# How expert rows come back to their tokens: shares applied at eviction, gathers that add, and two scatters into the output

## The reference, cut to what matters

```python
x = x + jnp.einsum('bsd,de->bse', merged, w_out[l])
h2 = rms_norm(x, norm2_gain[l])
x = x + hierarchical_moe(h2, ...)
...
top_val, top_idx = lax.top_k(e_sel_logits, TOP_K_IN_GROUP)
top_w = jax.nn.softmax(top_val, axis=-1) * g_w
combine_w = jnp.sum(jax.nn.one_hot(expert_id, N_EXPERTS) * top_w[..., None], axis=1)
...
hid = jax.nn.silu(a) * u * cs[:, :, None]
return jnp.einsum('nef,efd->nd', hid, w_down)
```

## Time and profile before

| | us |
|---|---|
| median of 3 runs | 1813.12 |
| lowest and highest | 1811.01, 1814.26 |
| profiled execution, its own time | 1811.73 |
| its span in the profile | 1809.9 |
| PE busy | 1748.1 |
| DVE busy | 1179.7 |
| ACT busy | 887.3 |
| POOL busy | 349.4 |

### The profile page before, as it was taken

One profiled execution on the slowest core, in us unless ns is written; L12 is line 12 of the kernel. 1 busy time (PEld: TensorE's weight loads), 2 busy tenths in 40 slices (PEclk: granted clock), 3 DMA queues, 4 the chain that ended last, 5 costly groups with the idle time before them and its releaser, 6 DMA issues.

```text
span 1809.9 us, 25327 instructions
## 1 busy us (share of the span) xinstructions
PE 1748.1 (97%) x10148; PEld 1438.6 (79%) x10148; DVE 1179.7 (65%) x1700; ACT 887.3 (49%) x1411; POOL 349.4 (19%) x228
## 2 busy tenths in 40 slices
PE   8999999999999999999999999999999999999993
PEld 6998788999897677788999776765568868888882
DVE  5575644554466655555776598586774466888896
ACT  5425434334334544334343365556653366878881
POOL 3323222001242322001000276310010030000001
PEclk8999999999999999999999999999999999999997
DMA  6203111323311212323222210112233349999984
GB/s 190 77 24 100 48 48 51 110 74 111 97 64 54 70 47 71 101 94 98 94 92 73 70 48 24 55 62 93 70 139 129 132 177 389 410 415 409 401 350 174
DMA packets 121279, 241.31 MB, mean 133 GB/s; under 512 B 9593, under 2 KB 101018, under 8 KB 115018
## 3 DMA queue, kind: packets, MB, share of 16 engines
q1 hardware_dynamic: 113786, 212.88, 33.2%
q0 software_dynamic: 4464, 16.25, 2.4%
q10 hardware_dynamic: 2912, 10.55, 1.4%
HBM read 223.41 MB, written 16.25 MB: 132 GB/s over the span
## 4 chain that ended last, share of the span: by engine, by line
PE 51%; DVE 5%; ACT 4%; issue 1%; DMA 1%; POOL 0%; POOLq 0%; ACTq 0%; DVEq 0%
PE acc L1409 15%; PE acc L880 10%; PE acc L1124 9%; PE acc L1149 7%; PE acc L1213 3%; PE acc L1227 2%; PE acc L1244 1%; PE acc L1235 1%; PE acc L1109 1%; PE acc L1393 1%; DVE upad L2751 1%; DVE qk L2751 1%; ACT v L2008 1%; PE acc L1031 0%; DVE qk L2749 0%
## 5 line engine op out<-in xcount | busy, mean ns | idle before, releaser
L880 PE MATMUL acc<-h_split,ring_split 128*128 128x264 f32 (+1 forms) x864 | 269.4, 312 | 0.0
L880 PEld LDWEIGHTS acc<-h_split,ring_split 128*128 128x128 f32 x864 | 162.3, 188 | 9.7
L1149 PE MATMUL acc<-ring_split,h_split 128*128 128x256 f32 x384 | 107.9, 281 | 0.0
L880 PE MATMUL acc<-h_split,qk_split 128*128 128x264 f32 (+1 forms) x288 | 92.6, 322 | 1.3 <-DVE ring_split L2255 1.3
L880 PE MATMUL acc<-ring_split,qk_split 128*128 128x264 f32 (+1 forms) x288 | 92.2, 320 | 0.0
L2255 DVE TENSOR_TENSOR ring_split<-ring,o_split 128x1024 fp32r<-128x1024 f32 (+1 forms) x32 | 44.8, 1415 | 64.3 <-ACT o_split L1570 64.2
L3067 POOL TENSOR_TENSOR latent<-latent 128x528 f32<-128x528 f32 x18 | 26.8, 1490 | 292.8 <-ACT latent L1565 292.4
L2255 DVE TENSOR_TENSOR ring_split<-ring,qk_split 128x1024 fp32r<-128x1024 f32 (+1 forms) x56 | 59.4, 1069 | 34.0 <-ACT qk_split L1570 34.0
L880 PE MATMUL acc<-h_split,krope_split 128*128 128x264 f32 (+1 forms) x240 | 79.4, 331 | 1.9 <-POOL ring_split L3081 1.9
L3081 POOL TENSOR_TENSOR ring_split<-ring,krope_split 128x1024 fp32r<-128x1024 f32 x20 | 48.1, 2406 | 152.4 <-ACT krope_split L1570 152.4
L880 PE MATMUL acc<-ring_split,krope_split 128*128 128x264 f32 (+1 forms) x240 | 77.0, 321 | 0.0
(11 more groups left out here) (599 smaller groups left out, 5579.2 us busy)
## 6 DMA issues: line engine op xcount, KB each, us to landing
ring<-in_w_in SPq DMA_DIRECT2D x64, 1024.0 KB, 5.3
ring<-in_w_expert_gate SPq DMA_DIRECT2D x10, 2048.0 KB, 11.1
ring<-in_w_expert_up SPq DMA_DIRECT2D x10, 2048.0 KB, 10.1
ring<-in_w_expert_down SPq DMA_DIRECT2D x10, 2048.0 KB, 10.6
ring<-in_w_out SPq DMA_DIRECT2D x12, 1024.0 KB, 5.2
y_rows<-gate ACTq DMA_DIRECT2D x16, 512.0 KB, 10.3
hres<-in_w_expert_up SPq DMA_DIRECT2D x3, 2048.0 KB, 10.3
qk<-in_w_expert_down SPq DMA_DIRECT2D x3, 2048.0 KB, 11.3
```

Source lines behind the costliest of these rows:

```text
L880: ins = nc.tensor.matmul(dst[0:rows_, half, 0:x.shape[1]], w[:, k, :], x, start=(k == 0 and i == 0), stop=(k == last and i == 2), skip_gro ...
L1149: ins = nc.tensor.matmul(dst[:, side, 0:WIDE], x[k][:, rows_], w, start=(k == 0 and part == 0), stop=(k == DC - 1 and part == 2), skip_gro ...
```

## The change: what it does

- The results are scaled by their shares when ACT evicts them: a factor for each slot (`R_WS`), made by eight matmuls on PE in turn 0 (`slot_weights`) and copied by DVE.
- The results of experts 0 to 13 (`FETCHED` of them) go to `y_rows` as before. `back_rows` is now worked out by DVE in turn 5 (`rows_fetched`); a result that isn't among these rows points to a tile of zeros. POOL, once the store of expert 13 has landed, issues four gathers for the tokens' first results and four for the second, each adding its rows to `x_tok` in place; a second one waits for the first of the same tile. SP then stores the four tiles to `out`. There is no DVE work in the combine.
- The results of experts 14 and 15 (`ADDED`) are not stored to `y_rows`. When the four stores to `out` have landed, POOL adds them from SBUF to rows of `out` by an indirect DMA that adds (a scatter), one after the other, each waited for. Their rows (`added_rows`) come from eight matmuls on PE in turn 4; the slots left free point to tokens of other experts, each a different one, with a share of 0.
- To that end the places of all tokens for all experts are worked out in turn 1. ACT evicts expert 13 at the start of turn 14, ahead of three `weights_up`. The hidden rows of expert 15 and its result get buffers of their own (`last_up`, `last_low`, `y_last`); the transposes of expert 15 come between the two halves of the down product of expert 14.
- The tile of zeros is one store instead of seven. The overflow loop also adds into `out`.

The core of the diff:

```diff
+ADDED = 2
+FETCHED = EXPERTS - ADDED
...
@@ SP
+            for i in range(QT):
+                sp.wait_ge(rows_back[i], 32)
+                sp.dma_start(out[0, i * P:(i + 1) * P, :], x_tok[:, i, :]).then_inc(stored, 16)
...
@@ PE
-                out_of_hidden(e)
+                out_of_hidden(e, range(1) if e == EXPERTS - 2 else range(2))
+
+            def slot_weights():
+                pe.wait_ge(dve_made, at(dve_made, "by_choice"))
+                for j in range(2):
+                    for i in range(QT):
+                        at_ = R_BY + 64 * j + 16 * i
+                        ins = nc.tensor.matmul(BANK["pick"][:, 0:EXPERTS], picks_whole[j][:, i, :].bitcast(F32), R[:, at_:at_ + EXPERTS],
+                                               start=(j == 0 and i == 0), stop=(j == 1 and i == QT - 1))
+                done(ins, "slot_weights")
+
+            def rows_added():
+                for x in range(ADDED):
+                    pe.wait_ge(dve_made, at(dve_made, ("added_pick", x)))
+                    for i in range(QT):
+                        ins = nc.tensor.matmul(BANK["pick"][:, 32 + x:33 + x], picks[x][:, i, :], late(K_TOKEN + i, 1),
+                                               start=(i == 0), stop=(i == QT - 1))
+                done(ins, "added_rows")
...
+                if e == 0:
+                    slot_weights()
+                if e == 4:
+                    rows_added()
                 down_of(e)
             hidden_of(EXPERTS - 1)
+            out_of_hidden(EXPERTS - 2, range(1, 2))
             down_of(EXPERTS - 1)
...
@@ ACT
                 act.wait_ge(psum_filled, at(psum_filled, ("y", e)))
-                if e:
+                if e == 0:
+                    act.wait_ge(dve_made, at(dve_made, "slot_weights"))
+                elif e <= FETCHED:
                     act.wait_ge(y_main, 16 * e)
-                evacuated(nc.scalar.activation(y_out, acc[:, 2, :, :].rearrange("p a b -> p (a b)"), ACT.Copy),
-                          ("y", e))
+                evacuated(nc.scalar.activation(y_out if e < EXPERTS - 1 else y_last,
+                                               acc[:, 2, :, :].rearrange("p a b -> p (a b)"), ACT.Copy,
+                                               scale=R[:, R_WS + e:R_WS + e + 1]), ("y", e))
+                if e >= FETCHED:
+                    return
...
+                if e == FETCHED:
+                    expert_out(e - 1)
                 weights_up(j + 2)
                 weights_up(j + 3)
                 weights_up(j + 4)
                 expert_gated(e + 1)
                 hidden_up(e)
-                if e:
+                if e and e < FETCHED:
                     expert_out(e - 1)
...
@@ DVE
                 weights_low(j + 6)
+                if e == EXPERTS - 2:
+                    hidden_low(EXPERTS - 1)
                 weights_low(j + 7)
-            hidden_low(EXPERTS - 1)
...
+                if e == 0:
+                    slot_weights()
+                elif e == 1:
+                    places_of_all()
+                elif e - 2 < ADDED:
+                    added_pick(e - 2)
+                elif e == 4:
+                    added_rows_kept()
+                elif e == 5:
+                    rows_fetched()
...
-            for i in range(QT):
-                dve.wait_ge(rows_back[i], 32)
-                for j in range(2):
-                    ins = stt(out=x_tok[:, i, :], in0=returned[:, 2 * i + j, :],
-                              scalar=R[:, R_WT + 4 * j + i:R_WT + 4 * j + i + 1], in1=x_tok[:, i, :],
-                              op0=ALU.mult, op1=ALU.add)
...
@@ POOL
+            pool.wait_ge(dve_made, at(dve_made, "back_rows"))
+            pool.wait_ge(act_evacuated, at(act_evacuated, ("x_tok", QT - 1)))
+            pool.wait_ge(y_zeroed, 16)
+            pool.wait_ge(y_main, 16 * FETCHED)
+            for j in range(2):
+                for i in range(QT):
+                    if j:
+                        pool.wait_ge(rows_back[i], 16)
+                    nc.gpsimd.indirect_dma_start(x_tok[:, i, :], None, y_rows,
+                                                 bass.IndirectOffsetOnAxis(back_rows[:, 4 * j + i:4 * j + i + 1], 0),
+                                                 compute_op=ALU.add).then_inc(rows_back[i], 16)
+
+            def add_rows(rows, source):
+
+                nc.gpsimd.indirect_dma_start(out[0], bass.IndirectOffsetOnAxis(rows, 0), source, None,
+                                             compute_op=ALU.add).then_inc(y_added, 16)
+
+            pool.wait_ge(stored, 16 * QT)
+            pool.wait_ge(dve_made, at(dve_made, "added_rows"))
+            for x in range(ADDED):
+                pool.wait_ge(act_evacuated, at(act_evacuated, ("y", FETCHED + x)))
+                add_rows(added_rows[:, x:x + 1], y_out if x < ADDED - 1 else y_last)
+                mark(y_added, None, 16)
+                pool.wait_ge(y_added, 16 * (x + 1))
...
-            pool.wait_ge(all_stored, 1)
-            for i in range(QT):
-                for j in range(2):
-                    nc.gpsimd.indirect_dma_start(returned[:, 2 * i + j, :], None, y_rows,
-                                                 bass.IndirectOffsetOnAxis(back_rows[:, 4 * j + i:4 * j + i + 1], 0))\
-                        .then_inc(rows_back[i], 16)
```

More of the change, by code:

```diff
@@ L1448, in out_of_hidden @@
                         ins.then_inc(first_half, 1)
-                done(ins, ("y", e))
+                if half == 1:
+                    done(ins, ("y", e))
             def weights_of(name):
@@ new lines, in _, with slot_weights, places_of_all @@
+            places = r(R_Q, QT, 16)
+            tokens_of = late(K_TOKEN, QT).unsqueeze(2).to_broadcast([P, QT, 16])
+            def slot_weights():
+                dve.wait_ge(psum_filled, at(psum_filled, "slot_weights"))
+                made(nc.vector.tensor_copy(R[:, R_WS:R_WS + EXPERTS], acc[:, 3, 1, 0:EXPERTS]), "slot_weights")
+            def places_of_all():
+                counts = R[:, R_P + 64:R_P + 80].unsqueeze(1).to_broadcast([P, QT, 16])
+                chain(stt(out=places, in0=r(R_P, QT, 16), scalar=-2.0, in1=tokens_of, op0=ALU.mult, op1=ALU.add))
+                chain(tt(places, places, counts, ALU.add))
+                chain(ts(R[:, R_V:R_V + 64], R[:, R_M:R_M + 64], -1.0, 1.0, ALU.mult, ALU.add))
+                chain(tt(R[:, R_Q:R_Q + 64], R[:, R_Q:R_Q + 64], R[:, R_V:R_V + 64], ALU.mult))
+                chain(tt(R[:, R_Q:R_Q + 64], R[:, R_Q:R_Q + 64], R[:, R_P:R_P + 64], ALU.add))
@@ new lines, in added_pick, with added_rows_kept, rows_fetched @@
+            def added_pick(x):
+                e = FETCHED + x
+                made(pick(picks[x], places[:, :, e:e + 1]), ("added_pick", x))
+            def added_rows_kept():
+                dve.wait_ge(psum_filled, at(psum_filled, "added_rows"))
+                made(nc.vector.tensor_copy(added_rows[:, :], acc[:, 3, 1, 32:32 + ADDED]), "added_rows")
+            def rows_fetched():
+                base, ok, row = (R[:, x:x + 8] for x in (R_S, R_S + 8, R_WT))
+                own, slot = late(K_TOKEN, 1), R[:, R_SLOT:R_SLOT + 8]
+                first = late(K_FIRST, 16).unsqueeze(1).to_broadcast([P, 8, 16])
+                chain(tt(r(R_KEY, 8, 16), r(R_SEL[0], 8, 16), first, ALU.mult))
+                chain(nc.vector.tensor_reduce(base, r(R_KEY, 8, 16), AX.X, ALU.add))
+                chain(ts(ok, slot, float(P), None, ALU.is_lt))
+                chain(stt(out=ok, in0=base, scalar=float(FETCHED * P), in1=ok, op0=ALU.is_lt, op1=ALU.mult))
+                chain(stt(out=row, in0=base, scalar=-float(FETCHED * P + 1), in1=slot, op0=ALU.add, op1=ALU.add))
+                chain(ts(row, row, own, None, ALU.subtract))
+                chain(tt(row, row, ok, ALU.mult))
+                chain(ts(row, row, own, float(FETCHED * P), ALU.add, ALU.add))
+                made(nc.vector.tensor_copy(back_rows[:, :], row), "back_rows")
@@ L3018, in _ @@
             with dve.If(tiles > 0):
+                which = R[:, R_TW:R_TW + 2 * QT].rearrange("p (i x) -> p i x", x=2)
+                chain(nc.vector.tensor_copy(which[:, :, 0:1], late(K_TOKEN, QT).unsqueeze(2)))
                 with dve.Fori(0, tiles) as k:
@@ L3022, in _ @@
                     mine = R[:, R_A:R_A + 4]
+                    chain(nc.vector.tensor_copy(which[:, :, 1:2], r(R_W, QT, 16)[:, :, bass.ds(expert, 1)]))
                     chain(nc.vector.tensor_copy(mine.unsqueeze(2), places[:, :, bass.ds(expert, 1)]))
@@ L3026, in _ @@
                     dve.wait_ge(psum_filled, at(psum_filled, ("pick", "+")))
+                    dve.wait_ge(y_added, at(y_added, ("y", "+"), back=1))
+                    chain(nc.vector.tensor_copy(R[:, R_WP:R_WP + 1], acc[:, 3, 1, 1:2]))
                     made(nc.vector.tensor_copy(rows_of[:, 0:1], acc[:, 3, 1, 0:1]), ("rows_of", "+"))
@@ L3181, in _ @@
             chain(nc.gpsimd.memset(padf[:, 0:D], 0.0))
```

(4 more changed lines are left out.)

100 lines of the change are left out of this document (33 added, 67 removed).

## The result

The change made the kernel slower. The changed kernel's median is 1819.3 us (1814.57 to 1823.52, 20 runs) against 1812.92 us (1808.9 to 1815.62, 20 runs) of the kernel before on the same chip: ratio 1.0035, 95% interval 1.0026 to 1.0043, or 6.4 us. The forecast was 1808.4 us and faster. The profiled execution took 1821.06 us, with a span of 1819.1.

What follows compares the result with a forecast made beforehand. PE bounds the kernel before 1770, then a 28.0 us combine tail from 1781.9. Sum: 1765.7 + 23.9 + 2.65 + 11.5 + 1.4 = 1805.15 against 1809.9, -4.7; for the median 1808.4 us, range 1798 to 1827.

Steps and rivals of the forecast that it cites:

- Part 1: PE's two groups of eight small matmuls, 1.0 us each, +2.0, and DVE's small operations in the turns, +0.5.
- Parts 2 and 3: Last two experts: PE waits 1.8 us at expert 15's up product, off the path; the first gather starts at 1763.2.
- Part 4: Eight adding gathers in the combine: 23.9 us from first start to last landing, POOL's issue rate not the limit.
- the same form: Gathers' span from first start to last landing: 2.9 fixed, eight transfers, and 1.4 for each out store mixed in.
- the rival of two passes: In gathers and scatters an adding row is held for two reads, 2.8 us per transfer: 1815.4 us, chance 0.2.
- The prediction's own sign: Combine gathers: landings 2.1 us apart would show the forecast right, 2.8 or more apart wrong.
- r: DMA engines' time for one adding 512 KB transfer, in gathers and scatters: taken as 2.1 us, break-even 2.58.
- Part 5: The last out store behind the gathers: 2.65 us, as now, but no longer the end.
- Part 6: Two adding scatters to out, one after the other: 5.75 us each, together 11.5.
- 2.9 + r: Each scatter priced in the gather's form, fixed 2.9 us plus the engines' time, with 0.75 for POOL's wake-up: 5.75.
- Part 7: The end behind the last landing: a register load and branch like ACT's 1.0 us and 0.4 left: 1.4.
- The slower rival: In gathers and scatters read, read and write follow one another, 4.2 us per transfer: 1829.4 us, chance 0.25.

Runs made afterwards that it cites:

- experiment 9: The changed kernel with one of slot_weights' eight small matmuls on TensorE instead of eight: 1814.87 us, ratio 1.0019 to the kernel before.
- experiment 6: The changed kernel with a buffer of its own for expert 13's result, so its eviction doesn't wait for expert 12's store: 1818.7 us, ratio 1.0033.
- experiment 3: The kernel before with its eight gathers in their old place but adding into x_tok, in place of DVE's adds: 1819.4 us, ratio 1.0041.
- experiment 1: The changed kernel with its eight combine gathers copying instead of adding: 1814.72 us, ratio 1.0016 to the kernel before.
- experiment 4: The kernel before with five extra 128x2048 subtractions on DVE beside its plain gathers: 1818.71 us, one execution.
- experiment 2: The changed kernel with its two scatters copying instead of adding: 1812.11 us, ratio 0.9992 to the kernel before.
- experiment 7: The changed kernel with POOL's register load of the overflow count moved ahead of the two scatters: 1819.43 us, ratio 1.0035 to the kernel before.
- experiment 8: The changed kernel with SP instead of POOL waiting for the last scatter: 1817.32 us, ratio 1.0026 to the kernel before.

## Why the prediction was wrong

The plan of the tail was right: a chain of POOL transfers, a DMA-bound stretch, two scatters, with expert 15's result off the path. Its sizes decided the sign. In the profiled execution the span was 14.0 us over the 1805.15 of the sum. Step by step:

- *Ahead of the experts*, 1.8: the granted clock of this execution, not the change.
- *Part 1*, 3.9 instead of 2.5: 3.5 for PE, beyond its end of 2.6, and 0.4 for DVE. The step "I take 1.0 each" failed, and its rows were misread. The eight matmuls of L1379 have f32r operands and leave one record each. The 1.00 of L1369 are not eight matmuls but four with f32 operands, which leave two records each (L1369 by its forms in the kernel before):

```profile
L1369 PE MATMUL acc<-o,ones x8: 262/262/276, 1479.3 to 1480.1; 128*128 128x64 f32 x2, 128*128 128x48 f32 x2, 128*128 128x32 f32 x2, 128*128 128x16 f32 x2
```

  The matmuls of the change have f32 operands, so a group of eight is 16 records and 1.84 to 1.86, nearly twice that 1.00 (experiment 9). The sum counted records as instructions where it should have counted what an instruction costs in its operand's type.
- *Parts 2 and 3*, 0.7 more: the store of expert 12 took 11.6 instead of 11.2, the eviction 0.1 more. PE's wait was 2.4 instead of 1.8 (0 to 2.5 in other executions with the same wait for the store) and, as said, not on the path (experiment 6).
- *Part 4*, 29.1 instead of 23.9, failed in two steps. "1.5 x 1.4 = 2.1": adding costs 2.45 to 2.6 by the same form with nothing beside it (experiment 3), toward the rival of two passes with 2.8. And "POOL's issue rate isn't the limit": the 1.39 of the earlier trace rows was taken for the expert stage, but that gather met only the last 0.58 us of a subtraction. Beside a row of them a gather holds POOL 1.85 to 3.6 (experiments 1, 4, 6), and a row of the kernel before, from the start of the expert stage, showed it:

```profile
1491.24 2.31 POOL L3199 DMA_INDIRECT latent<-h_rows,rows_of  x1 [4.84 <-PE acc L1393]
```

  The two overlap. First start to last landing is 16.9 plain with DVE mostly idle, 24.9 plain beside the subtractions, 26.7 adding with DVE idle and 27.9 to 29.1 with both, which is why taking away the adding alone gives back 3 to 4 us of the gathers' time and not the 9.8 of experiment 3. The prediction's own sign came true: the eight landings are about 3.0 apart, not 2.1. An r at the break-even of 2.58 would have left no room for any other miss.
- *Part 5*, 3.9 instead of 2.65: the last out store, issued at 1798.7, runs beside the one before it, issued at 1795.2 and landed at 1801.1; in the kernel before the others had landed by then (1806.7 against 1806.88).
- *Part 6*, 12.95 instead of 11.5 from the last out store's landing to the last scatter's. The form "2.9 + r", with 5.0 for an adding transfer, fell short of the 6.2 measured, by more than r alone (2.9 + 2.6 = 5.5); a plain one lands in 3.3 (experiment 2).
- *Part 7*, 3.5 instead of 1.4: the step took ACT's end, and the end stood behind POOL (experiments 7, 8).

The excesses are 1.8 + 1.4 + 0.7 + 5.2 + 1.25 + 1.45 + 2.1 = 13.9. Without the first, 12.1 are the change's own, and -4.7 + 12.1 = 7.4 compares with the 6.4 of the medians; the gathers of this execution are 1 us longer than in three of the four others.

By r alone the likeliest rival was that of two passes, with "no change". Its 29.5 for the gathers and 12.9 for the scatters are within 0.5 us of the measured 29.1 and 12.95, but that is in part luck: an adding gather costs 1.6 to 1.9 plain ones and not 2, POOL's waits for DVE fill the difference, and a scatter's 6.2 is more than 2.9 + 2.8. The time came out above that rival through PE's share of part 1 and through parts 5 and 7, for none of which the prediction had an end wide enough, and, in the profiled execution, through the clock ahead of the experts. The slower rival's mechanism, three passes in a row with r from 2.94 on, isn't what happened.

The rule that the prediction cites for two passes, from the Trainium skill ("Collectives: The Full Stack", section "The bandwidth ceiling: the fold count and why AG ≠ RS ≠ AR"), is given there for the adding step of a collective: half the rate of a copy. The traces here are near it (1.6 to 1.9 copies), not at it.

What stays open: whether POOL waits for a lock, as the page of the Trainium skill on SBUF has it, or for something else that DVE's instruction holds; and how the factor of adding splits between reads and writes. No run tried either.

## What to carry to other kernels

A transfer that adds is no free addition: price it at nearly two copies, and compare it with the adds that it saves on an engine that may be idle. Before a transfer issued by GpSimd is moved to an earlier stage, look at what VectorE does there, since each gather can have to wait for the VectorE instruction that is running, and at which other transfer in that stage is on the path. A chain of dependent small waits at the end of a program is priced by the engine that waits last.

## What the runs showed of the hardware that had not been expected

- An adding gather of 512 KB into SBUF takes 2.45 to 2.6 us of the DMA engines (1.4 plain, by the same form) at a share of 0.95 and 195 GB/s, and holds POOL 1.53 to 1.59 (0.94) with nothing beside it. An adding scatter of 512 KB to DRAM lands after 6.0 to 6.3 us (3.3), and holds POOL 1.56 to 1.62 (1.0).
- A gather that is issued while DVE runs an instruction lets go of POOL 0.79 to 0.87 us after that instruction's end (188 plain gathers), or 1.40 to 1.53 after it (41 adding ones). Subtractions of 128x2048 in a row so double and more what a gather costs POOL; DVE's adds of 128x1024, 1.3 each, make it up to 1.6; ACT's copies of 128x2048 change nothing.
- Behind the last landing, a program's end took 3.5 us where POOL waited for it and 1.45 where SP did.
- Behind PE's 2.36 us of waiting, a pair of matmuls took 1.07 us instead of 0.62, with a granted clock of 0.50 from 1772 to 1774, which is 1.2 GHz. It needn't come: in experiments 1 and 2 PE waited 2.48 and 2.44 at the same place, and the clock stayed at 1.00.
